# Gate and up projections of a feed-forward block by Strassen's seven block products, in two token passes, on one Trainium2 core

## What is computed

```python
x = x + mix @ lp["w_out"]
h = rms_norm(x, lp["norm_ffn"])
x = x + (jax.nn.silu(h @ lp["w_gate"]) * (h @ lp["w_up"])) @ lp["w_down"]
x = x + jax.nn.sigmoid(rms_norm(x, lp["norm_ple"]) @ lp["w_ple_gate"]) * (pe @ lp["w_ple_proj"])
```

## Time and profile before

| | |
|---|---|
| median of three executions | 1849.56 us |
| the profiled execution, its time | 1852.12 us |
| its span, first to last instruction | 1850.3 us |
| TensorE, matmuls | 1762.0 us busy (95%), x10268 |
| TensorE, weight loads (beside the matmuls) | 1557.7 us (84%) |
| VectorE (DVE) | 1028.0 us (56%) |
| ScalarE (ACT) | 527.5 us (29%) |
| GpSimd (POOL) | 389.3 us (21%) |
| granted TensorE clock, mean | 0.989 of full |

### The profile page before, as it was taken

How to read it: one execution, slowest core, us unless ns; L and a number is a source line. 1 busy time by engine, 2 the same in 40 slices (tenths; PEclk the granted TensorE clock), 3 DMA queues, 4 the chain that set the end, 5 groups by cost and what they waited for, 6 DMA issues and landing times.

```text
span 1850.3 us, 27171 instructions
## 1 busy us (share of the span) xinstructions
PE 1762.0 (95%) x10268; PEld 1557.7 (84%) x10268; DVE 1028.0 (56%) x1659; ACT 527.5 (29%) x1040; POOL 389.3 (21%) x262
## 2 busy tenths in 40 slices
PE   7999898999999998889999999999999999999998
PEld 6999786667888887768798898998998998998886
DVE  5476885775888888756534334334334244244543
ACT  5202355555443443634321111111111111111111
POOL 2204693221655455513300000000000000000000
PEclk9999998999999999989999999999999999999999
DMA  6401000011421222120021111111111111112011
GB/s 188 125 6 39 14 1 0 1 34 33 138 53 52 64 62 66 46 97 1 8 84 46 34 44 37 44 45 45 45 45 45 45 45 45 45 68 77 29 43 41
DMA packets 108947, 91.89 MB, mean 50 GB/s; under 512 B 25571, under 2 KB 97792, under 8 KB 108845
## 3 DMA queue, kind: packets, MB, share of 16 engines
q1 hardware_dynamic: 106851, 89.63, 16.0%
q10 hardware_dynamic: 2002, 1.03, 0.2%
HBM read 84.73 MB, written 6.26 MB: 49 GB/s over the span
## 4 chain that ended last, share of the span: by engine, by line
PE 79%; DVE 8%; POOL 4%; ACT 3%; SPq 3%; issue 3%; DMA 1%; ACTq 0%; POOLq 0%; DVEq 0%
PE ps L1945 22%; PE ps L1947 22%; PE ps L1946 22%; POOL stats L751 2%; PE ps L2356 2%; PE ps L536 1%; PE ps L2187 1%; DVE arena L1410 1%; PE ps L2140 1%; SPq L624 1%; PE ps L1952 1%; DVE arena L1772 1%; PE ps L2144 1%; PE ps L2248 1%; DVE arena L1644 1%
## 5 line engine op out<-in xcount | busy, mean ns | idle before, releaser
L1945 PE MATMUL ps<-h_hi,w_hi 128*128 128x384 f32 (+1 forms) x1056 | 345.6, 327 | 0.0
L1946 PE MATMUL ps<-h_lo,w_hi 128*128 128x384 f32 (+1 forms) x1056 | 345.4, 327 | 0.0
L1947 PE MATMUL ps<-h_hi,w_lo 128*128 128x384 f32 (+1 forms) x1056 | 345.4, 327 | 0.0
L1867 DVE TENSOR_TENSOR gate_s<-gate_s,ps 128x384 f32<-128x384 f32 (+1 forms) x66 | 35.1, 532 | 337.8 <-PE ps L1947 337.8
L885 POOL TENSOR_TENSOR arena<-arena,mhalf 128x32 f32<-128x32 f32 x32 | 177.1, 5535 | 144.3 <-DVE arena L1776 144.3
L1946 PEld LDWEIGHTS ps<-h_lo,w_hi 128*128 128x128 f32 x1056 | 198.5, 188 | 0.5
L1945 PEld LDWEIGHTS ps<-h_hi,w_hi 128*128 128x128 f32 x1056 | 198.5, 188 | 0.5
L1947 PEld LDWEIGHTS ps<-h_hi,w_lo 128*128 128x128 f32 x1056 | 198.5, 188 | 0.0
L1879 DVE TENSOR_TENSOR arena<-arena,ps 128x512 f32<-128x512 f32 x187 | 128.3, 687 | 123.9 <-PE ps L1947 109.7
L530 POOL TENSOR_TENSOR stats<-stats,mhalf 128x1 f32<-128x1 f32 (+1 forms) x18 | 9.8, 543 | 888.4 <-DVE stats L520 888.4
L1945 PE MATMUL ps<-cw_hi,pT_hi 128*128 128x288 f32 x512 | 161.0, 314 | 10.2 <-DVE pT_lo L1691 9.4
(11 more groups left out here) (324 smaller groups left out, 3579.8 us busy)
## 6 DMA issues: line engine op xcount, KB each, us to landing
arena<-in_cache_ckv SPq DMA_DIRECT2D x128, 128.0 KB, 2.0
w_raw<-in_w_gate SPq DMA_DIRECT2D x22, 512.0 KB, 3.9
w_raw<-in_w_up SPq DMA_DIRECT2D x22, 512.0 KB, 5.1
arena<-in_x_prompt SPq DMA_DIRECT2D x16, 512.0 KB, 5.6
w_uk<-in_w_down SPq DMA_DIRECT2D x11, 512.0 KB, 3.5
w_uv<-in_w_down SPq DMA_DIRECT2D x11, 512.0 KB, 4.2
gw_raw<-in_w_in SPq DMA_DIRECT2D x8, 512.0 KB, 5.8
w_out<-in_w_out SPq DMA_DIRECT2D x1, 4096.0 KB, 13.3
```

The lines of the kernel that those rows point to most:

```text
L1867: ch.link(nc.vector.tensor_tensor(gate_s[:, c], gate_s[:, c], ps[:, 2 * b + 1, 0:n], ALU.mult))
L1945: mm(out, left[0], right[0], start=start, stop=False)
L1946: mm(out, left[0], right[1], start=False, stop=False)
L1947: return mm(out, left[1], right[0], start=False, stop=stop)
```

## The change

The change replaces, for the gate and up products, eight block products by seven (Strassen's scheme in Winograd's form). Per group and matrix the weight is seen as 2 x 2 blocks (two halves of the 1024 rows, two slices of 128 columns) and the tokens as 2 x 2 blocks (two halves of the rows, two halves of the tokens). Four weight blocks are replaced by sums of blocks (`weight_sums`, GpSimd, 128x512 each), four token blocks by sums (`token_sums`, GpSimd, once a pass), and the results are put together by seven additions (`add`, VectorE, one input in PSUM).

The tokens are taken in two passes, c = 0 with the upper prompt tiles and the samples (blocks of 288 columns), c = 1 with the lower tiles (256), and all weights are loaded and split anew in the second. A unit (c, g, u) is the seven products of gate (u = 0) or up (u = 1), each 4 x 3 matmuls. TensorE's order is gate of group g, downs of group g - 1, up of group g. Each product has one set of operand buffers, so each of its parts for the next unit is written when its product of this unit is done. Silu is taken from SBUF, the high part of the activation moves to ScalarE, and every `low_w` handles 512 elements a row. The last four `h_T` and their norms move between the units of the last group of pass 0. The order of the tiles at the end is that of `END_TILES`.

```diff
-DOWNS = 2 * TILES + 1
-DOWN_ORDER = [(t, h) for t in range(6) for h in range(2)] + [(TILES, 0)] + [(t, h) for t in range(6, TILES) for h in range(2)]
...
+HALVES = ((SEQ // 2, 288), (0, 256))
+DOWN_ORDER = ([(TILES, 0)] + [(t, h) for t in range(4, TILES) for h in range(2)], [(t, h) for t in range(4) for h in range(2)])
+DOWNS = [len(o) for o in DOWN_ORDER]
+PRODUCTS = 7
+DONE_AT = {0: 1, 2: 2, 3: 3, 1: 4, 4: 5, 5: 6, 6: 7}
...
+PRODUCT_BANK = {0: 0, 2: 1, 3: 2, 1: 3, 4: 4, 5: 5, 6: 1}
...
-OUT_TILES = [7, 6, 0, 1, 2, 3, 4, 5, TILES]
...
+OUT_TILES = [7, 6, 5, 4, TILES, 0, 1, 2, 3]
+END_TILES = [4, 5, 6, 7, TILES, 0, 1, 2, 3]
...
+            def load_gu(g, u):
+                sp.dma_start(w_raw[u], w_v[u][:, :, bass.ds(2 * P * g, 2 * P)]).then_inc(s_(f"gu_loaded{u}"), 16)
...
+            def token_sums(c, places):
+                if c == 0:
+                    pool.wait_ge(s_("c_hT"), FFN_TILES)
+                else:
...
+                if 1 in places:
+                    nc.gpsimd.tensor_tensor(t_part(c, 1), t_part(c, 5), t_part(c, 4), ALU.subtract).then_inc(s_("w_pool"), 1)
+                if 2 in places:
+                    nc.gpsimd.tensor_tensor(t_part(c, 4), t_part(c, 4), t_part(c, 0), ALU.subtract).then_inc(s_("w_pool"), 1)
+                if 3 in places:
+                    pool.wait_ge(s_("w_pool"), base + 2)
+                    nc.gpsimd.tensor_tensor(t_part(c, 2), t_part(c, 5), t_part(c, 4), ALU.subtract).then_inc(s_("w_pool"), 1)
+                if 4 in places:
+                    pool.wait_ge(s_("w_pool"), base + 3)
+                    pool.wait_ge(s_("h_split"), PRODUCTS * c + TOKEN_AT[3])
+                    nc.gpsimd.tensor_tensor(t_part(c, 6), t_part(c, 3), t_part(c, 2), ALU.subtract).then_inc(s_("w_pool"), 1)
+            def weight_sums(c, g, u):
...
+                pool.wait_ge(s_(f"gu_loaded{u}"), 16 * (g + GROUPS * c + 1))
+                if isinstance(done, int) and done == 0:
+                    pool.wait_ge(s_("m_xT"), NT)
+                else:
+                    pool.wait_ge(s_("w_split"), PRODUCTS * done)
+                nc.gpsimd.tensor_tensor(w_diff, w_part(u, 0), w_part(u, 4), ALU.subtract).then_inc(s_("w_pool"), 1)
+                nc.gpsimd.tensor_tensor(w_part(u, 4), w_part(u, 4), w_part(u, 6), ALU.add).then_inc(s_("w_pool"), 1)
+                pool.wait_ge(s_("w_pool"), w_sum(c, g, u, 2))
+                nc.gpsimd.tensor_tensor(w_back, w_part(u, 4), w_part(u, 0), ALU.subtract).then_inc(s_("w_pool"), 1)
+                pool.wait_ge(s_("w_pool"), w_sum(c, g, u, 3))
+                nc.gpsimd.tensor_tensor(w_rest, w_part(u, 3), w_back, ALU.subtract).then_inc(s_("w_pool"), 1)
...
+            def high_w(c, g, u, q):
...
+                if q == 0:
+                    act.wait_ge(s_(f"gu_loaded{u}"), 16 * (g + GROUPS * c + 1))
+                if not first:
+                    act.wait_ge(s_("prod_done"), PRODUCTS * (done - 1) + DONE_AT[q])
+                if q in (1, 4, 2, 5):
+                    act.wait_ge(s_("w_pool"), w_sum(c, g, u, {1: 1, 4: 2, 2: 3, 5: 4}[q]))
+                nc.scalar.activation(w_hi_r[q].rearrange("p (k c) -> p k c", c=P), w_part(u, q), ACT.Copy).then_inc(s_("w_hi_ready"), 1)
...
+            def unit_act(c, g, u, following, wd=None, turn=None):
+                n, k = HALVES[c][1], unit_at(c, g, u)
...
+                def silu(f, h, place):
+                    if u == 0:
+                        act.wait_ge(s_("sum_ready"), 7 * k + place)
+                        at = gate_s[:, f, h * n:(h + 1) * n]
+                        nc.scalar.activation(at, at, ACT.Silu).then_inc(s_("silu_ready"), 1)
+                act.wait_ge(s_("prod_done"), PRODUCTS * k + DONE_AT[0])
+                if not first:
+                    act.wait_ge(s_("sum_ready"), 7 * k)
+                    if u == 0:
+                        act.wait_ge(s_("glu_ready"), NU + 4 * (g + GROUPS * c))
+                nc.scalar.activation(p_one[:, 0:n], ps[:, PRODUCT_BANK[0], 0:n], ACT.Copy).then_inc(s_("part_copied"), 1)
+                if following:
+                    high_w(*following, 0)
+                if wd:
+                    high_wd(*wd[0:2], wd[2][0:1])
+                if following:
+                    high_w(*following, 2)
+                    high_w(*following, 3)
...
+                if following:
+                    high_w(*following, 1)
+                silu(0, 0, 2)
+                if wd:
+                    high_wd(*wd[0:2], wd[2][1:2])
+                if following:
+                    high_w(*following, 4)
+                silu(1, 1, 4)
+                if following:
+                    high_w(*following, 5)
+                silu(0, 1, 6)
+                if following:
+                    high_w(*following, 6)
+                silu(1, 0, 7)
+                if u == 1:
...
+                        act.wait_ge(s_("dn_done"), down_at(c, g))
+                    for j, (f, h) in enumerate(((0, 0), (1, 1), (0, 1), (1, 0))):
+                        act.wait_ge(s_("glu_ready"), NU + 4 * (g + GROUPS * c) + j + 1)
+                        nc.scalar.activation(a_hi_r[f][:, h * n:(h + 1) * n], gate_s[:, f, h * n:(h + 1) * n], ACT.Copy).then_inc(s_("act_high"), 1)
...
+            def low_w(c, g, u, q):
+                dve.wait_ge(s_("w_hi_ready"), PRODUCTS * unit_at(c, g, u) + DONE_AT[q])
+                nc.vector.tensor_tensor(w_lo_r[q].rearrange("p (k c) -> p k c", c=P), w_part(u, q), w_hi[q].rearrange("p (k c) -> p k c", c=P),
+                                        ALU.subtract).then_inc(s_("w_split"), 1)
...
+            def unit_dve(c, g, u, following, wd=None, gains=()):
+                n, k = HALVES[c][1], unit_at(c, g, u)
...
+                G = g + GROUPS * c
+                def add(out, part, product, place, needs):
+                    dve.wait_ge(s_("prod_done"), PRODUCTS * k + DONE_AT[product])
+                    if needs:
+                        dve.wait_ge(s_("sum_ready"), 7 * k + needs)
+                    nc.vector.tensor_tensor(out[:, 0:n], part[:, 0:n], ps[:, PRODUCT_BANK[product], 0:n], ALU.add).then_inc(s_("sum_ready"), 1)
+                def out_of(f, h, part):
+                    return part if u else gate_s[:, f, h * n:(h + 1) * n]
+                def mult(f, h, part, place):
+                    if u:
+                        dve.wait_ge(s_("sum_ready"), 7 * k + place)
+                        out = gate_s[:, f, h * n:(h + 1) * n]
+                        nc.vector.tensor_tensor(out, out, part[:, 0:n], ALU.mult).then_inc(s_("glu_ready"), 1)
+                if following:
+                    low_w(*following, 0)
+                if wd:
+                    low_wd(*wd[0:2], wd[2][0:1])
...
+                dve.wait_ge(s_("part_copied"), k + 1)
+                if not (isinstance(k, int) and k == 0):
+                    dve.wait_ge(s_("sum_ready"), 7 * k)
+                    dve.wait_ge(s_("glu_ready"), NU + 4 * G)
+                add(p_two, p_one, 2, 1, 0)
+                if following:
+                    low_w(*following, 2)
+                if u == 0 and not first:
+                    dve.wait_ge(s_("aT_ready"), 4 * G)
+                if u == 1:
+                    dve.wait_ge(s_("silu_ready"), 4 * G + 4)
+                add(out_of(0, 0, p_one), p_one, 3, 2, 1)
+                if following:
+                    low_w(*following, 3)
+                mult(0, 0, p_one, 2)
+                add(p_three, p_two, 1, 3, 1)
+                if following:
+                    low_w(*following, 1)
+                if wd:
+                    low_wd(*wd[0:2], wd[2][1:2])
+                add(out_of(1, 1, c_sum), p_three, 4, 4, 3)
+                add(p_two, p_two, 4, 5, 3)
+                mult(1, 1, c_sum, 4)
+                if following:
+                    low_w(*following, 4)
...
+                add(out_of(0, 1, p_two), p_two, 5, 6, 5)
+                if following:
+                    low_w(*following, 5)
+                mult(0, 1, p_two, 6)
+                add(out_of(1, 0, p_three), p_three, 6, 7, 4)
+                if following:
+                    low_w(*following, 6)
+                mult(1, 0, p_three, 7)
+                if u == 1:
+                    if c == 0:
+                        dve.wait_ge(s_("glu_ready"), NU + 4 * G + 3)
+                        for f in range(2):
+                            ch.link(nc.vector.tensor_copy(a_s[f], gate_s[:, f, 2 * n - NS:2 * n]))
+                    for j, (f, h) in enumerate(((0, 0), (1, 1), (0, 1), (1, 0))):
+                        dve.wait_ge(s_("act_high"), 2 * NT + 4 * G + j + 1)
+                        w = slice(h * n, (h + 1) * n)
+                        nc.vector.tensor_tensor(a_lo_r[f][:, w], gate_s[:, f, w], a_hi[f][:, w], ALU.subtract).then_inc(s_("aT_ready"), 1)
+            def down_add(c, g, e):
+                dve.wait_ge(s_("dn_done"), down_at(c, g) + e + 1)
+                t, h = DOWN_ORDER[c][e]
```

(54 more changed lines are left out.)

## The result

The kernel after took 1915.95 us, the median of four runs (1908.69 to 1918.25), beside 1848.27 us (1845.78 to 1852.52) for the kernel before: 1.036 times as long (95% interval 1.032 to 1.039). The forecast was 1864 us with a range of 1830 to 1890. The sign was right and the size was not: the change costs 66 to 68 us, where 14 were forecast. The profiled execution took 1916.08 us, with a span of 1914.3.

The account below looks back on a forecast made before the run. The prediction took TensorE's matmul streaming to bound the feed-forward part. Span: 1850.3 - 62.7 (columns saved) + 42 (waits in the loops) + 35 (edges) = 1864.6 us; median forecast 1864 us, range 1830 to 1890.

Parts of the forecast that it names:

- waits in the loops: TensorE's waits for VectorE in the group loops: 2.7 us a group in pass 1, 1.7 in pass 0, 42 us.
- the edges: Waits at the start, the change of passes and the end, all estimates: 35 us (20 to 50).
- TensorE as the bound, columns as its time: Feed-forward part lasts as long as its matmuls stream; fewer columns save their full time, 62.7 us in all.
- The rate at 256 and 288 columns: In the seven products, 0.1164 us a matmul at 256 columns and 0.1314 at 288, read from earlier profile rows.
- the down piece: In each group's downs, 1.37 us a piece; the 17 pieces a group are only moved.
- the turns: In gate units, VectorE and GpSimd instructions follow one another: 0.8 us for each of four sums, 3.2 us a unit.
- where 0.25 were charged: In the gate unit, VectorE waits 0.25 us for ScalarE, whose silu stands in line between two high parts.
- ScalarE's 7.5 of 9.8 us of work: ScalarE has some 7.5 us of work a unit, of 9.8; costed at nothing.
- "Long waits on ScalarE": Sign that the forecast is wrong: long waits on ScalarE, which it had put at nothing.
- "I take the clock to stay full": TensorE's clock stays at 1.00 throughout, so nothing was added for it.
- D: Rival: whole lengths lost in the turns, or each VectorE semaphore step 30 ns dearer; 1900 us, slower; chance 0.11.
- a whole length lost each time: Upper bound for the loops' waits: each VectorE-GpSimd meeting blocks for the other's full instruction, 73 us.

Follow-up runs that it names:

- experiment 2: The kernel after with nearly all VectorE, ScalarE and GpSimd work left out in the loops over the groups, semaphores and TensorE's instructions kept; one run, 1843.9 us.
- Experiment 1: The kernel after with GpSimd's weight sums in the loops cut to 2 of 128 columns, 1839.09 us, or to 64 of 128, 1861.94 us.
- experiment 5: The kernel after with a second pair of buffers for two up-unit sums, so GpSimd makes three of its four sums earlier; 1866.59 us.
- Experiments 3 and 4: In 3, throwaway matmuls before pass 1's down pieces in the kernel after, 1908.65 us; in 4, TensorE waits before down pieces in the kernel before, 1896.45 us.
- 6: The kernel of experiment 5 with token sums made later, second-group early sums at their old place, and last units splitting all down-weight quarters; 1856.3 us.
- the half sums: The kernel after with half of each of GpSimd's weight sums left out in the loops over the groups; 1861.94 us.

## Why the prediction missed

The forecast was 14 us of span more, and it is 64: a miss of 50. By the periods of the groups, 20 of them are waits in the loops and 12 to 13 the stream; 5 lie outside the part, and the last 12 at the edges.

**TensorE as the bound, columns as its time.** Right. A unit came to 84 x 0.1329 = 11.2 and 84 x 0.119 = 10.0 us, where 11.04 and 9.78 were forecast.

**The rate at 256 and 288 columns.** Too low by 1 to 2%, because rows 6 are from other stages with operands at other places, and the down piece was taken from the kernel before, whose `a_lo` stood elsewhere. 1848 x 0.0015 + 1848 x 0.0026 + 1056 x 0.0051 = 13 us. For the down pieces the cause is shown. For the products only a part of the pattern is: in the kernel of experiment 2 each of the seven products has its own rate, the same in all units of pass 1 (0.117 for the last, 0.118 to 0.120 for the others), which points to place too but was not tried.

**The waits in the loops: the step that failed.** The forecast had 42 us for them, 2.7 for a group of pass 1 and 1.7 in pass 0. Measured against the groups without sums, it is 3.7 in pass 1 (4.0 to 4.2 where the clock falls) and 2.5 in pass 0, 62 us in all. The list of idle time has 42.4 in the loops and 34.7 at the edges, where 42 and 35 were forecast; that it agrees to the microsecond is luck, since it leaves out what lies between idle time and time from start to start, and the way was only half right. In pass 1 the turns cost 2.45 us a gate unit, where 3.2 were charged; but ScalarE's wait for `w_back` passed 1.5 us on to VectorE, where 0.25 were charged. The forecast had taken from ScalarE's 7.5 of 9.8 us of work that it costs nothing. It was not its work but its order: it stands behind one late sum with the other high parts queued behind. "Long waits on ScalarE" was one of the forecast's own signs of being wrong, and VectorE's come to 34 us in the loop of pass 1. In pass 0 the turns cost 4.3 us, where 3.2 were charged. Experiment 1 shows that GpSimd's sums cause all of it, and experiment 5 that the time at which they are made does; how turns and chain share it stays open.

**"I take the clock to stay full".** This failed too: zero in the sum, and 17 us of excess in stretches at half clock. The argument was the earlier trace rows, a clock of 1.00 in a stretch in which TensorE never paused; the forecast itself then put pauses into that stretch. Experiments 3 and 4 show that the pauses bring the clock down, and not the load. But it explains little of the miss: in pass 1's groups some 3 us (0.4 to 0.5 in six of them), and the 7.3 of experiment 3 with what else it changed. What the six falls at the edges, 8 us of excess, cost in the end was not tried. The Trainium skill ("TensorE: Matmul & The Clock Gate", Part 1, on the clock gate) says that the clock has two levels and that activity releases the throttle; the windows here agree, with 0.50 in the middle of a fall and 1.00 behind it. The page of the kernel before could have warned. Its clock digits have an 8 in two slices, both among those where the earlier trace rows have TensorE at 8 tenths and not 9:

```profile
PEclk9999998999999999989999999999999999999999
```

**The rivals.** D, at 1900, was nearest, for another reason than its own: the sums did not cost 1.2 us each in pass 1, and the loops' waits were 62 us and not 73.

The Trainium skill's rule ("SBUF — State Buffer", section "Who interferes with whom") is that the pair of ports that VectorE and GpSimd share is an exclusive lock. The trace agrees at every length: the second to begin waits until the first is through, less 0.13 us. Beside sums of 1024 elements 2.02 and 2.14 us were lost with 2.15 and 2.28 left to run, beside those of 512 elements 0.54 to 1.09 with 0.68 to 1.23 left. (One exception stands in the last section.) Where the forecast read the rule as a whole length lost each time (its 73 us), it is what is left of the other's instruction that is lost, by whichever engine comes second.

**Costed at nothing otherwise.** The doubled loads held: behind 990 us the lists of waits have none on a load, at a DMA share of 0.22 to 0.29; loads of 1024 KB landed in 5.3 and 5.4 us.

## What to carry to other kernels

When a change puts pauses of 2 to 3 us into a stretch in which TensorE never paused, expect matmuls at half clock behind most of them, and ask who sets the pace: here it cost 1.6 us a pause where TensorE did, and 0.4 to 0.5 where another engine did. Compare the periods of groups with and without the effect; the excess of the matmuls alone overstates it. An engine that hands out work in a fixed order is late when one of its inputs is late, however idle it is; follow each new producer through every queue that reads it. Helper work on GpSimd costs by when it meets VectorE: 49 of 68 us came back through a second pair of buffers.

## What the runs showed of the hardware

The place of a stationary operand changes the rate of a stream that seemed to be limited by its columns alone: 0.2331 or 0.2268 us for 512 columns, by the place of one of two tiles, with nothing else running. What it is about the place, its distance or its address, is open.

The same pause of 2.62 us was followed by half clock in nine groups and by full clock in two.

VectorE's instructions with two operands in SBUF and GpSimd's sums wait for one another by a rule that holds for all 191 lengthened ones (splits, low parts, products with gate) of four kernels (the kernel after and those of experiments 5, 6 and of the half sums): the later one loses what is left of the other less 0.11 to 0.13 us. It works in both directions. In each group of pass 1's loop GpSimd's first sum began 0.16 us after a product of VectorE, and four subtractions that followed it without a gap went through unlengthened, while the sum took 2.75 us for 1.30.

Small instructions pay most for this. The copies of the sample columns, 128 x 64, in the groups of the kernel after (busy us, mean ns):

```profile
L2133 DVE COPY arena<-gate_s 128x64 f32<-128x64 f32 x22 | 25.5, 1157 | 0.4
```

1157 ns on average, where they took 189 on average in the kernel of experiment 5, with the sums out of their way.
